# Second attention of a two-block transformer kernel: stationary values, outputs by feature, weights divided before their transposes

## The chip, the cores and the metric

The kernel runs on one core of one Trainium2 chip, as one launch. The metric is the device time of that launch in microseconds (us), taken as the median of several executions. Lower is better.

The engines are TensorE (PE in the profile; its weight loads are PEld), VectorE (DVE), ScalarE (ACT), GpSimd (POOL) and SyncE (SP), which only starts DMAs here. They run their own instruction lists, in the order of the program, and meet at semaphores.

## The reference

The program is a stack of two blocks over 512 tokens of 1024 features. This case is about the second attention of the first block, which comes after the first feed-forward network:

```python
kvf = rms_norm(h, kv_norm) @ w_kvf            # keys, values: 16 heads of 64; forget gates
c_sh = jnp.cumsum(log_sigmoid(kvf[..., 2 * B_WIDTH:] + b_f), axis=1)

def fox_mixer(xn, w_q, w_o, k, v, c):
    q = (xn @ w_q).reshape(B, T, B_HEADS, HEAD_DIM)
    for i in range(T // BLK):                 # BLK = 128 queries, keys up to the block's end
        s = q_block . k * scale + (c_q - c_k)
        s = jnp.where(causal, s, NEG)
        p = jax.nn.softmax(s, axis=-1)
        outs.append(p @ v[:, :q1])
    return concatenate(outs).reshape(B, T, B_WIDTH) @ w_o
```

All of it is float32. A dense product is made as three products of rounded parts (high by high, high by low, low by high); the products of softmax weights and values are plain float32.

## The kernel before, in words

**Layout.** Activations stand by feature: a tile of 128 partitions is 128 features, its 512 columns the tokens (KD = 8 such tiles make 1024 features). Scores stand by query: 128 queries in the partitions, up to 512 keys in the columns.

**Tasks.** The 16 heads go in 8 pairs. A pair has four tasks, one for each block `tb` of 128 queries, in the order 0, 2, 3, 1 (`MIXED`), which see 1, 3, 4 and 2 blocks of keys. That makes 32 tasks `t`. For each task and each of its two heads `g`:

- `pair_scores` (L1259, L1262): the scores of both heads, with the two heads on the two halves of the array's rows; results in banks 0 and 1.
- `pair_max` (L1326, L1330): VectorE adds the mask, takes the maximum and scales it.
- `pair_probs` (L1304): ScalarE takes the exponential and sums it. The weights are not divided yet.
- `pair_turn` (L1272): PE transposes the weights, a 128 by 128 block at a time, into banks 4 and 5. ScalarE copies head 0's (L1316), VectorE head 1's (L1351), into `b_PT`.
- `pair_values` (L1281): the transposed weights (128 keys by 128 queries) are the stationary operand and the values (128 keys by 64) the moving one. The result is by query, 128 by 64 a head, in bank 6 or 7.
- `pair_out` (L1335, L1337): VectorE takes the reciprocal of the sums and multiplies the result by it into `b_o`, which stands by token.

**Order on PE** (`b_pe`): in step t it runs the scores of task t+1, two blocks `k` of a key or query projection (`kq_fill`, half 0), the transposes of task t, two more blocks (`kq_fill`, half 1), and the values of task t-1. A block is three products of 128 by 128 by 512. `kq_fill` prepares the keys and queries of the next pair, two steps ahead (`KQ_AHEAD`), and has work in steps up to 25 only. VectorE and ScalarE follow the same steps; GpSimd makes the low part of each projection (L1244) and splits the weight units that come by DMA into a high and a low part (L497, L503). Three units fit into `parts`, so the split of a unit waits for the products of the unit three places ahead of it.

**After the last task** `flip_pe` (L1083) transposes `b_o` in 8 chunks of four blocks to stand by feature, `flip_act` (L1089) makes the high part and `flip_dve` (L1094) the low part (`b_fm`). Then `out_pe` makes the 8 output products of `w_o`, 24 matmuls each (L522 in all dense products); the first three are made together, block by block (`together=PARTS`), the others one after another. `out_dve` and `out_act` take them, form the norm and add to `h`.

**Ahead of the tasks** `mixb_pe` makes the first half of the values (`b_v0`), then `pre_sums_pe` (L653), which sums squares that VectorE has added (L663, L664), then the product of the forget gates (`b_f`, 24 matmuls), then `pre_columns_pe` (L676), which needs the reciprocal root (L657 on ScalarE, L669 on VectorE), then the second half of the values (`b_v1`), whose bank 7 comes free only after ScalarE's copy of those columns (L681).

## Time and profile before

| | us |
|---|---|
| median of 3 executions | 2281.19 |
| lowest, highest | 2278.80, 2281.82 |
| the profiled execution's own time | 2286.73 |
| its span, first to last instruction | 2284.9 |
| PE busy | 2157.0 (94%) |
| DVE, ACT, POOL busy | 1446.2, 591.0, 1157.0 |

The profile is of one execution. A span of an engine says that it worked, not that anybody waited for it. The chain of waits is followed back from the last instruction; "issue" in it is time in which the engine waited for nothing that the profile shows. The granted clock is that of TensorE, as a share of 2.4 GHz. The second attention, with what is ahead of it and its output products, takes the span from about 651 to 924 us.

### The profile page before, as it was taken

The page shows a single profiled execution, that of the slowest core. Times are in us where ns is not written, and L with a number is a line of the kernel's source. Part 1 is how long each engine was busy: PE and PEld are TensorE (multiplying, and loading weights), DVE is VectorE, ACT ScalarE, POOL GpSimd, SP SyncE. Part 2 cuts the span into 40 slices and gives each one's busy share as a digit, 9 for nine tenths or more (in the row PEclk, how much of TensorE's full clock was granted, in tenths as well). Part 3 has the DMA queues.
Part 4 walks back from the last instruction along what each step waited for, and adds up shares of the span by engine and source line. Part 5 has one row for each costly group of instructions (what it writes and reads, how often), then busy time and mean ns, then how long its engine had stood idle before and what let it go on. Part 6 is the DMA issues. An engine that isn't in the chain of part 4 may idle for free.

```text
span 2284.9 us, 34060 instructions
## 1 busy us (share of the span) xinstructions
PE 2157.0 (94%) x14118; PEld 1796.5 (79%) x14118; DVE 1446.2 (63%) x1894; ACT 591.0 (26%) x1215; POOL 1157.0 (51%) x658
## 2 busy tenths in 40 slices
PE   7999899999989998999999989989989978999998
PEld 5867788888868887788888758877888867888886
DVE  7455778567685454778767788768665664621622
ACT  2143321022133332321022142255434222200200
POOL 6711466765746443466665542543400354656654
PEclk9999999999989999999999999989989998999999
DMA  5310233532622111223433531112100112323321
GB/s 186 111 36 19 74 100 121 166 101 93 214 69 82 47 47 50 83 95 132 158 98 107 202 140 38 63 57 75 56 3 4 52 36 64 108 86 108 95 92 65
DMA packets 55769, 201.94 MB, mean 88 GB/s; under 512 B 6560, under 2 KB 6816, under 8 KB 54720
## 3 DMA queue, kind: packets, MB, share of 16 engines
q1 hardware_dynamic: 52272, 187.21, 25.2%
q0 software_dynamic: 1840, 9.60, 1.1%
q10 hardware_dynamic: 1504, 2.95, 0.5%
q8 instruction: 112, 1.84, 0.3%
q14 instruction: 41, 0.34, 0.0%
HBM read 194.76 MB, written 4.19 MB: 87 GB/s over the span
## 4 chain that ended last, share of the span: by engine, by line
PE 82%; DVE 11%; ACT 3%; issue 2%; POOL 1%; DMA 0%; SPq 0%; DVEq 0%; POOLq 0%; ACTq 0%
PE bank L522 64%; PE bank L1281 1%; PE bank L2636 1%; PE bank L988 1%; PE bank L2632 1%; PE bank L964 1%; DVE big L1513 1%; PE bank L2900 1%; PE bank L2621 1%; POOL parts_r L503 1%; PE bank L1709 1%; PE bank L1272 1%; PE bank L1521 1%; DVE big L663 1%; DVE h L798 1%
## 5 line engine op out<-in xcount | busy, mean ns | idle before, releaser
L522 PE MATMUL bank<-xn_r,parts_r 128*128 128x512 f32 (+1 forms) x2928 | 910.0, 390 | 32.0 <-DVE mix_r L746 13.2
L522 PE MATMUL bank<-big_r,parts_r 128*128 128x512 f32 x3208 | 926.9, 392 | 1.9 <-POOL parts_r L503 1.9
L503 POOL TENSOR_TENSOR parts_r<-ring,parts_r 128x1024 fp32r<-128x1024 f32 x293 | 739.9, 2525 | 24.4
L497 POOL TENSOR_SCALAR parts_r<-ring 128x1024 fp32r<-128x1024 f32 x293 | 346.5, 1182 | 792.5 <-PE bank L522 780.3
L522 PEld LDWEIGHTS bank<-big_r,parts_r 128*128 128x128 f32 x3208 | 603.0, 189 | 135.2 <-issue 5.7
L522 PEld LDWEIGHTS bank<-xn_r,parts_r 128*128 128x128 f32 x2928 | 551.5, 190 | 156.3 <-issue 35.2
L873 ACT ACTIVATE big<-bank,small 128x512 f32<-128x512 f32 x88 | 68.4, 780 | 411.0 <-DVE big L917 251.3
L902 DVE TENSOR_TENSOR bank<-bank,nb 128x512 f32<-128x512 f32 x88 | 61.3, 699 | 143.3 <-PE bank L522 143.2
L3167 DVE SCALAR_TENSOR_TENSOR h<-bank,vecs,h 128x512 f32<-128x512 f32 x24 | 17.9, 750 | 173.4 <-PE bank L522 173.4
L3241 DVE TENSOR_TENSOR big<-big 128x512 f32<-128x512 f32 x32 | 83.0, 2595 | 70.3 <-ACT big_r L3222 70.3
L533 DVE TENSOR_TENSOR big_r<-big,big_r 128x512 fp32r<-128x512 f32 x76 | 105.8, 1394 | 0.4
L522 PE MATMUL bank<-parts_r,xn_r 128*128 128x384 f32 x352 | 92.1, 343 | 6.5 <-ACT big L2025 3.5
L3046 POOL TENSOR_TENSOR big<-big 64x384 f32<-64x384 f32 x11 | 9.7, 878 | 158.6 <-PE bank L2664 147.3
L1513 DVE SCALAR_TENSOR_TENSOR big<-cst,vecs,big 128x1024 f32<-128x1024 f32 x42 | 88.0, 2122 | 2.5 <-DMA cst<-mod_w 1.6
L522 PE MATMUL bank<-mix_r,parts_r 128*128 128x512 f32 x208 | 82.0, 394 | 0.0
L917 DVE TENSOR_TENSOR big<-big 128x512 f32<-128x512 f32 x44 | 80.9, 1839 | 0.0
L3220 ACT ACTIVATE big<-bank 128x512 f32<-128x512 f32 x32 | 19.1, 597 | 220.1 <-PE bank L522 220.1
L522 PEld LDWEIGHTS bank<-parts_r,xn_r 128*128 128x128 f32 x352 | 64.9, 193 | 8.8 <-ACT big L2025 3.8
L910 DVE SCALAR_TENSOR_TENSOR big<-bank,small,big 128x510 f32<-128x510 f32 x88 | 65.9, 749 | 3.1
L696 ACT ACTIVATE nb<-mix 128x512 f32<-128x512 f32 x32 | 20.2, 632 | 175.3 <-DVE mix L786 105.4
L907 DVE SCALAR_TENSOR_TENSOR big<-bank,small,big 128x511 f32<-128x511 f32 x88 | 65.2, 741 | 0.5 <-ACT big L873 0.5
L522 PE MATMUL bank<-h_r,parts_r 128*128 128x512 f32 x160 | 63.1, 394 | 0.0
(443 smaller groups left out, 2901.8 us busy)
## 6 DMA issues: line engine op xcount, KB each, us to landing
ring<-weights SPq DMA_DIRECT2D x295, 512.0 KB, 3.5
cst<-mod_w SPq DMA_DIRECT2D x48, 512.0 KB, 4.1
cst<-consts SPq DMA_DIRECT2D x2, 1280.0 KB, 8.1
h<-x SPq DMA_DIRECT2D x8, 256.0 KB, 6.5
h_store<-h POOLq DMA_DIRECT2D x8, 256.0 KB, 2.3
big<-consts POOLq DMA_DIRECT2D x2, 1024.0 KB, 8.3
h<-h_store POOLq DMA_DIRECT2D x1, 2048.0 KB, 8.0
out<-mix SPq DMA_DIRECT2D x8, 256.0 KB, 2.2
```

What stands on the lines that cost most here:

```text
L497: pool.tensor_scalar(rounded(unit_parts(u)[0]), ring[:, u % RING], 1.0, 0.0, ALU.mult, ALU.add)\
L503: pool.tensor_tensor(rounded(lo), ring[:, u % RING], value(hi), ALU.subtract).then_inc(part_ready, 1)
L522: mm = pe.matmul(ps, rounded(w[a]), rounded(x[b]), start=(start and n == 0), stop=(stop and n == 2))
L533: dve.tensor_tensor(rounded(lo[:, k]), x[:, k], value(hi[:, k]), ALU.subtract).then_inc(sem(done), 1)
L663: link(dve, dve.tensor_tensor(pre_sq[:, 0:half], pre_sq[:, 0:half], pre_sq[:, half:2 * half], ALU.add))
L873: act.activation(cv[:, i % 4], bank[i % 4][:, :], ACT.Identity, bias=gain(f"cb{l}", 2 * KH * s + i), scale=gain(f"cw{l}2", 2 * KH * s + i))\
L902: dve.tensor_tensor(bank[i % 4][:, :], bank[i % 4][:, :], rstd, ALU.mult).then_inc(sem(st + "_sc"), 1)
L907: link(dve, dve.scalar_tensor_tensor(out=c[:, 1:T], in0=ps[:, 0:T - 1], scalar=gain(f"cw{l}1", w), in1=c[:, 1:T], op0=ALU.mult, op1=ALU.add))
L910: dve.scalar_tensor_tensor(out=c[:, 2:T], in0=ps[:, 0:T - 2], scalar=gain(f"cw{l}0", w), in1=c[:, 2:T], op0=ALU.mult, op1=ALU.add).then_in ...
L917: dve.tensor_tensor(ff_lo[:, j], ge[:, j % 2], cv[:, (2 * j + 1) % 4], ALU.mult).then_inc(sem(st + "_ff"), 1)
L1513: ins = dve.scalar_tensor_tensor(out=acc, in0=w, scalar=c, in1=acc, op0=ALU.mult, op1=ALU.add)
L3241: dve.tensor_tensor(ff2_lo[:, f], ff2_lo[:, f], ff2_lo[:, f], ALU.mult).then_inc(sem("mlp_sq"), 1)
```

## The change

1. **Values are stationary.** `pair_values` now takes the values (128 keys by 64) as the stationary operand and the transposed weights (128 keys by 128 queries) as the moving one. The two heads take the two halves of the array's columns, so that their results stand in partitions 0 to 63 and 64 to 127 of one bank, by feature. The four tasks of a pair write the four quarters of one bank (6 or 7 by turns).
2. **ScalarE divides ahead of the transposes.** A query is now a column of the result, so the division can't be made there. VectorE takes the reciprocal (`pair_norm`) right after its maximum of the same task, and ScalarE multiplies the weights by it in place (`b_scaled`), 128 by w a head, ahead of the transposes. `pair_out` is gone.
3. **No flip.** The 32 transposes, 8 high and 8 low parts behind the last task are gone. Each pair's bank is copied by ScalarE as it closes: pairs 0 to 5 (`B_STASH`) into `b_o`, since `xn` is in use until the last projection; their high parts are made by ScalarE in steps 26 to 28 and their low parts by GpSimd (`stash_lo_pool`); pairs 6 and 7 get their parts from ScalarE and VectorE directly.
4. **Output products start in the last steps.** `tail_fill` puts block k = t - 27 of output products 0 and 1 into steps 27 to 32, where `kq_fill` has nothing. The rest follows in `b_out_pe`, product after product; the three are no longer made together. GpSimd's split of unit 2 of `w_o` moves behind the six low parts.
5. **`b_f` ahead of `pre_sums_pe`.**

```diff
 def pair_turn(pe, t):
-    pe.wait_ge(*after("b_probs", 2 * t + g + 1))
+    pe.wait_ge(*after("b_scaled", 2 * t + g + 1))
 def pair_values(pe, t):
-    ps = grab(pe, 6 + t % 2, *after("b_rows", t + 1))
-    for g in range(2):
-        pe.wait_ge(*after("b_pt_dve" if g else "b_pt_act", t + 1))
-        for kb in range(tb + 1):
-            mm = pe.matmul(ps[:, g * HD:(g + 1) * HD], b_PT[t % 2][g][:, kb * P:(kb + 1) * P],
-                           b_v[:, kb, (2 * pair + g) * HD:(2 * pair + g + 1) * HD], ...)
+    if t % PAIR == 0:
+        grab(pe, 6 + pair % 2, *(after("b_stash", pair + 1) if pair < B_STASH else after("b_fm", pair + 1)))
+    ps = bank[6 + pair % 2]
+    pe.wait_ge(*after("b_pt_act", t + 1))
+    pe.wait_ge(*after("b_pt_dve", t + 1))
+    for kb in range(tb + 1):
+        for g, r in enumerate(half_rows):
+            mm = pe.matmul(ps[r, tb * P:(tb + 1) * P], b_v[:, kb, head * HD:(head + 1) * HD],
+                           b_PT[t % 2][g][:, kb * P:(kb + 1) * P], ...)
...
+def tail_fill(pe, t, half):
+    k = t - SPLIT_FROM - 1          # SPLIT_FROM = 26
+    if k >= 0:
+        b_out_product(pe, half, k)  # waits for b_fm k+1, then 3 matmuls
...
 def pair_probs(act, t):
     for g in range(2):
         act.activation(p_, p_, ACT.Exp, ..., accum_out=b_stat(t, 2)[:, g:g + 1])
+    act.wait_ge(*after("b_norm", t + 1))
+    for g in range(2):
+        act.activation(p_, p_, ACT.Copy, scale=b_stat(t, 3)[:, g:g + 1]).then_inc(sem("b_scaled"), 1)
...
+def pair_norm(dve, t):
     dve.wait_ge(*after("b_probs", 2 * t + 2))
-    link(dve, dve.reciprocal(b_stat(t, 3), b_stat(t, 2)))
-    dve.wait_ge(*after("b_values", t + 1))
-    dve.tensor_tensor(b_o[...], bank[6 + t % 2][:, 0:P], ..., ALU.mult)
+    dve.reciprocal(b_stat(t, 3), b_stat(t, 2)).then_inc(sem("b_norm"), 1)
 def b_dve(dve):
     for t in range(b_n):
         if t + 1 < b_n:
             pair_max(dve, t + 1)
+            pair_norm(dve, t + 1)
...
 # mixb_pe
-    pre_sums_pe(pe, "b")
     # product of b_f, 24 matmuls
+    pre_sums_pe(pe, "b")
     pre_columns_pe(pe, "b")
...
     b_pe(pe)
-    flip_pe(pe, "b", b_o, KD, "b_rows", lambda c: PAIR * (c + 1))
-    out_pe(pe, "b", "b_o", KD, b_oT, ("b_fm", 0))
+    b_out_pe(pe)
...
 # block.gpsimd
+    for pair in range(B_STASH):
+        stash_lo_pool(pool, pair)
-    split_units(pool, UNITS["b_kq"] + PARTS + 2 * KD, UNITS["hy"])
+    split_units(pool, UNITS["b_kq"] + PARTS + 2 * KD - 1, UNITS["hy"])
```

Three places show how the instructions stand. All line numbers of the kernel after are one to some eighty higher for the same code.

PE ahead of the tasks, from the last products of `b_v0` (parts_r as stationary of 128x512) on; 653 or 654 is `pre_sums_pe`, 676 or 677 `pre_columns_pe`, `big_r,parts_r x24` is `b_f`. Before:

```order
L522 MATMUL bank<-parts_r,big_r 128x512 x96
L653 MATMUL bank<-big,base 128x512
L522 MATMUL bank<-big_r,parts_r 128x512 x24
L676 MATMUL bank<-base,nb 128x1 x4
L522 MATMUL bank<-parts_r,big_r 128x512 x96
```

Now:

```order
L523 MATMUL bank<-parts_r,big_r 128x512 x96
L523 MATMUL bank<-big_r,parts_r 128x512 x24
L654 MATMUL bank<-big,base 128x512
L677 MATMUL bank<-base,nb 128x1 x4
L523 MATMUL bank<-parts_r,big_r 128x512 x96
```

The gates' product stands ahead of the sum of squares instead of behind it.

PE in step 29 of the tasks, from the scores of task 30 (512 keys) to those of task 31 (256 keys). Before:

```order
L1259 MATMUL bank<-nb_r,cst_r 128x512 x2
L1262 MATMUL bank<-big_r 128x512 x2
L1262 MATMUL bank<-xn_r,big_r 128x512 x2
L1262 MATMUL bank<-big_r,xn_r 128x512 x2
L1272 MATMUL bank<-base,big 128x128 x6
L1281 MATMUL bank<-big 128x64
L1281 MATMUL bank<-big,nb 128x64
L1259 MATMUL bank<-nb_r,cst_r 128x256 x2
```

Now:

```order
L1263 MATMUL bank<-big_r,xn_r 128x512 x2
L523 MATMUL bank<-xn_r,parts_r 128x512
L523 MATMUL bank<-big_r,parts_r 128x512
L523 MATMUL bank<-xn_r,parts_r 128x512
L1273 MATMUL bank<-base,big 128x128 x6
L523 MATMUL bank<-xn_r,parts_r 128x512
L523 MATMUL bank<-big_r,parts_r 128x512
L523 MATMUL bank<-xn_r,parts_r 128x512
L1286 MATMUL bank<-big 64x128
L1286 MATMUL bank<-nb,big 64x128
L1260 MATMUL bank<-nb_r,cst_r 128x256 x2
```

A block of output product 0 stands ahead of the transposes and one of output product 1 behind them; the values' results are 64 partitions by 128 columns instead of 128 by 64.

ScalarE in the tasks of one pair (1304 or 1338 the exponentials, 1316 or 1383 the copies of transposed weights, 1239 or 1240 a projection's high part). Before:

```order
L1304 ACTIVATE big,stat<-big,stat 128x128 x2
L1304 ACTIVATE big,stat<-big,stat 128x384 x2
L1316 ACTIVATE big<-bank 128x128
L1304 ACTIVATE big,stat<-big,stat 128x512 x2
L1316 ACTIVATE nb<-bank 128x384
```

Now:

```order
L1338 ACTIVATE big,stat<-big,stat 128x384 x2
L1343 ACTIVATE big<-big,stat 128x384 x2
L1383 ACTIVATE big<-bank 128x128
L1338 ACTIVATE big,stat<-big,stat 128x512 x2
L1343 ACTIVATE big<-big,stat 128x512 x2
L1383 ACTIVATE nb<-bank 128x384
L1240 ACTIVATE big_r<-xn 128x512
L1347 ACTIVATE big<-bank 128x512
```

Each task has two multiplications more (L1343), and each pair one copy of a whole bank (L1347).

## Rows read from the trace of the kernel before

**Rows 1.** Windows of PE: us, busy (instructions), granted clock, DMA share, GB/s.
```profile
657.00:662.00 5.00, 0.03 (x1) 0.82 0.15 59
...
664.00:667.00 3.00, 3.00 (x9) 0.50 0.03 10
```
**Rows 2.** The chain of waits ahead of the tasks: start, us, what.
```profile
661.97 2.05 PE bank L653 x2
664.01 6.94 PE bank L522 x24
670.96 0.80 PE bank L676 x8
...
672.93 39.96 PE bank L522 x168
```
**Rows 3.** The timeline of ScalarE and VectorE there, with idle time before.
```profile
664.05 0.69 ACT L657 ACTIVATE nb<-bank,small 128x512 f32<-128x512 f32 x1 [12.40 <-PE bank L653]
664.77 3.35 DVE L669 RECIPROCAL nb<-nb 128x512 f32<-128x512 f32 x1 [2.95 <-ACT nb L657]
```
**Rows 4.** The chain in the tasks of one pair.
```profile
776.42 1.73 PE bank L1281 x16
...
779.05 1.59 PE bank L522 x6
780.64 0.22 PE bank L1272 x2
780.86 1.39 PE bank L522 x6
782.25 0.84 PE bank L1281 x8
...
787.84 0.39 PE bank L1281 x4
...
792.74 1.28 PE bank L1281 x12
...
798.03 1.73 PE bank L1281 x16
```
**Rows 5.** The chain at two groups of f32 matmuls with 512 moving columns.
```profile
1316.88 1.82 PE bank L1685 x4
...
1581.51 1.00 PE bank L2374 x8
```
**Rows 6.** Groups by form in the tasks (712 to 878): busy us, mean ns | idle.
```profile
L1330 DVE TENSOR_SCALAR stat<-stat 128x2 f32<-128x2 f32 x32 | 19.0, 594 | 1.1
L1326 DVE CUSTOM_DVE_ANT_0 big<-bank,cst 128x512 f32<-128x512 f32 x16 | 10.4, 689 | 8.2 <-PE bank L1262 8.2
L1335 DVE RECIPROCAL stat<-stat 128x2 f32<-128x2 f32 x31 | 4.8, 154 | 0.0
L1304 ACT ACTIVATE big<-big,stat 128x512 f32<-128x512 f32 x16 | 11.4, 716 | 22.7 <-DVE stat L1330 22.7
L1239 ACT ACTIVATE big_r<-xn 128x512 fp32r<-128x512 f32 x14 | 8.8, 630 | 21.3 <-DVE xn L1234 21.3
```
**Rows 7.** PE's waits from 850 to 925 us: total, times, longest.
```profile
PE bank L522 <- POOL parts_r L503: 2.4, 1, 2.4
PE bank L1272 <- ACT nb L1316: 1.3, 1, 1.3
PE bank L522 <- DVE big_r L1094: 1.2, 1, 1.2
PE bank L1272 <- ACT big L1316: 0.9, 2, 0.5
```
**Rows 8.** The chain at the output products.
```profile
877.50 15.26 PE bank L522 x66
...
896.46 27.50 PE bank L522 x120
```
**Rows 9.** One line's instructions, durations min/median/max.
```profile
L1244 POOL TENSOR_TENSOR xn_r<-xn,big_r x16: 1272/1288/1298, 703.5 to 854.1; 128x512 fp32r<-128x512 f32 x16
```

## What the change would do, predicted before it ran

> **What bounds the kernel now.** PE is busy for 94% of the span, so I read the chain of waits first, and in the stretch that the change touches. It has three parts. *Ahead of the tasks* PE stands still: 5.1 us without work while VectorE adds squares, and the granted clock is at half (1.2 GHz) from 664 to 667 [rows 1]; the sum of squares, the gates' product at 0.289 us a matmul, the columns and the copy by ScalarE then follow each other until `b_v1` starts at 672.93 [rows 2]. *In the tasks* with projections to fill in (steps 0 to 25) the chain never leaves PE: the reader should see each row begin where the last one ends, and a pair come round in 798.03 - 776.42 = 21.6 us [rows 4]. ScalarE and VectorE wait there, so work on them is free as long as their own chain fits into PE's step. *In the tail* (steps 26 on, no `kq_fill`) PE waits: three times for copies of transposed weights, then 1.2 us for the low parts behind the flip, then 2.4 us for GpSimd's split of `w_o` unit 3, which could start only when product 0 closed, and product 0 closed late because the first three are made together [rows 7, 8].
>
> **Durations.** The sum is made against the profiled execution (2286.73 us, span 2284.9). The median, 2281.19, is 5.5 us (0.24%) lower; I take the difference of the sum off the median. A dense matmul on a warm clock is 27.50/120 = 0.229 us [rows 8].
>
> **Part 5, `b_f` ahead of the sum of squares.** Now PE idles from 657 to 661.97 [rows 1, 2]. With the change the 24 matmuls stand there at full clock: 24 x 0.229 = 5.5, to 662.5. The sum of squares took 2.05 on the low clock [rows 2], about 1.0 on the full one: 663.4. From there to the columns stand ScalarE's root (0.69) and VectorE's reciprocal (3.35) [rows 3]: 667.5. Then columns 0.8 and the same 1.2 to the start of `b_v1`: 669.5 against 672.93, a gain of 3.4. PE now idles 4.1 us there, which a half clock may follow. Before, half of `b_f` ran at it and is repaid already in the 5.5; a half clock over the first 3 us of `b_v1`, as long as the stretch in [rows 1], would give back 1.5, and twice that length 3. Bounds 0.4 and 3.4; I take **2.3**, nearer the upper one, since `b_v1` started on a lowered clock before as well.
>
> **Part 1, values.** Before, one logical product of 128x128 weights and 64 columns is two records of 0.107 us; a pair has 40 of them: 1.73 + 0.84 + 0.39 + 1.28 = 4.24 us [rows 4]. After, the moving operand has 128 columns. No row has this form. The bounds: a full f32 record with 512 columns takes 1.82/4 = 0.455, so one with 128 takes 0.114; eight records of the same 512 columns, on four narrow column groups over the same rows, took 1.00 us together instead of 3.6 [rows 5]. So column groups do run beside each other. Two heads side by side give 20 x 0.112 = 2.24 us a pair; one after the other 40 x 0.112 = 4.5. I take the first, since [rows 5] shows the overlap outright.
>
> There is a price. The same six dense matmuls take 1.39 us behind transposes and 1.59 behind the row-split scores [rows 4]: leaving a divided array costs 0.2 us. The change adds a second array shape to each step, so one more switch, x4 a pair = 0.8 us. Bounds for it 0.1 (only the drain, the gates small) and 0.3. So a pair costs 2.24 + 0.8 = 3.04 and gains 1.2.
>
> The Trainium skill speaks against this part: TensorEngine Tiling, Tiling Modes (Key Properties), says that changing the tiling mode drains the engine. By that rule, the trace agrees: 1.59 against 1.39. With a free change of mode this sum would be 6.4 us better over 32 tasks.
>
> With PE as the bound in 26 of 32 steps: 6.5 pairs x 1.2 = 7.8. At the start the first transposes wait for the reciprocal and two multiplications more, about 0.8. Together **7.0**. The bounds of the switch (0.1 and 0.3, that is 2.6 either way over 26 steps) go into the range.
>
> **Part 2, division.** ScalarE gets two multiplications a task. The nearest row is a copy out of SBUF of 512 columns, 0.63 [rows 6]; by width 0.63, 0.52, 0.41, 0.30, twice each, 3.7 us a pair, with a bank copy 4.3, on an engine that has a row's wait of 22.7 us ahead of the 512-key exponentials alone. Its load is hidden. The wait that is added is the question: VectorE now waits for the exponentials, with its copy for head 1 and `kq_take` queued behind; ScalarE waits for the reciprocal with its copy for head 0 behind. For a task with 512 keys, from the scores' end: hand-over 0.15; VectorE 2 x 0.69 + 0.17 = 1.5; exponentials 2 x 0.72; reciprocal 0.15 and 0.2 of hand-overs; multiplications 2 x 0.63: 4.9 us [rows 6]. PE meanwhile runs fill 1.6, transposes 0.7, fill 1.4, values 0.7, next scores 1.0, fill 1.6: 7.0 us, by rows like [rows 4]. It fits with 2.1 to spare. I cost it at nothing there; the cover is `kq_fill`. In the tail that cover is gone.
>
> **Parts 3 and 4, the tail**, from the scores of task 28 on. Work taken off PE: 32 transposes, 3.5 us; values of tasks 26 to 31, 6.9 to about 4.8 with their switches; against five switches back to dense products, 1.0. That is 4.6 less. The 192 output matmuls are the same 44 us, 36 of them moved forward. Waits taken off: all of [rows 7] and short ones at the flip, some 6. Waits added: ScalarE needs for each task of the tail its two exponentials, 0.36 for the reciprocal, two multiplications, one copy and up to two high parts, 3.5 to 5 us a step, where PE's step has 1.4 of fill now. The first tail block waits for the first low part: exponentials of task 27 (1.0), reciprocal (0.4), multiplications (0.8), copy (0.6), high part (0.6), then GpSimd's low part, 1.29 by [rows 9]: 4.7 us behind the end of the previous ScalarE step, of which PE covers 1.3 (scores and the end of values): wait 3.4. Steps 30 and 31 wait 2.2 and 1.8 for copies behind 512- and 256-key multiplications. Together 7.4. Unit 3 of `w_o` is split while products 1 and 2 run, so the 2.4 is gone. Net 4.6 + 6 - 7.4, about **3.2** gained. Behind the output products nothing changes but bank numbers.
>
> **Sum.** 2.3 + 7.0 + 3.2 = 12.5 us. Own time 2286.7 - 12.5 = 2274.2; median 2281.2 - 12.5, rounded to **2269**.
>
> **Rivals.**
>
> *Heads one after the other.* If the streams of two column groups didn't overlap, 20 slots a pair would be 40: 2.24 us more, x6.5 = 14.6, and 1.5 more in the tail where PE waits anyway: 2269 + 14.6 = 2283.6, no change within 0.2%. Against it is the 1.00 us in [rows 5]. 7%.
>
> *The division's chain becomes the bound.* VectorE's small multiply by the scale (L1330) took 0.594 us in the mean [rows 6] where its work is 0.17: something holds it up, by 0.4 in the mean, and GpSimd's ops of 1.3 to 2.4 us run beside it. In the trace this costs ScalarE time only, now it is in the chain. Say the chain is longer than 4.9 by x in every step. Below x = 2.1 only the six tail steps feel it, from there all. Break-even with before is at about 2.1 (6 x 2.1 = 12.6); slower by over 0.2% from about x = 2.3: 26 x 0.2 + 6 x 2.3 = 19, where 17 is needed. With x = 2.6 it is 26 x 0.5 + 6 x 2.6 = 28.6, the time 2298. For it speaks that three engines now hand over in turn; against it that x = 2.6 is six times the mean hold-up. 5%.
>
> The Trainium skill gives that hold-up a cause: SBUF — State Buffer, Who interferes with whom, says that VectorE in a two-port mode, which a `tensor_scalar` may enter, and GpSimd exclude each other for a whole instruction. By that rule, the mean of 0.594 agrees, and the added reciprocal (0.154 in the mean, never held up) does not add a second such place.
>
> *The tail gives its gain back.* More than 7.4 us of waits, or a clock at half after one or two of them, 1.5 us lost for each stretch as long as that in [rows 1], on top of longer waits: 2273 to 2277, and, if the blocks start no earlier at all and the change so doesn't do what it says, 2272. 22%.
>
> *Switches are cheap* (0.1) and `b_v1` starts warm: 3.2 more in the steps 0 to 31 and 1.1 ahead, with shorter tail waits: 2261 to 2264. 12%.
>
> *Forecast*: 2265 to 2273, 54%.
>
> **How the numbers follow.** The range must leave out at most 2 in 10. From 2261 to 2278 it holds the forecast, the cheap switches and the tail's case. Outside are the serial heads, the chain, and some overshoot. 0.2% is 4.6 us, about what a measurement of this kernel can tell from no change. Faster by more than that means under 2276.6: forecast, cheap switches and most of the tail's case, 0.85. Within it: serial heads and the rest of the tail's, 0.10. Slower: the chain, 0.05.
>
> **What the profile after would show.** Values: a block of keys in about 0.22 us instead of 0.43; a pair's period near 20.4 us instead of 21.6, with PE still in every row of the chain. Where `kq_fill` is, no PE wait for the transposes' inputs (releaser L1343); such rows there would be the second rival. Output block 0 waiting for GpSimd about 3 us. `b_v1` starting some 3 us sooner behind the last `b_v0` product. Between the last values and output product 7 no wait for GpSimd. The prediction is wrong if the pair's period stays at 21.6 or PE waits in the steps 0 to 25.

## The result, and the profile after

The changed kernel takes 2271.8 us (median of six, 2269.6 to 2274.5), the kernel before 2281.5 us (median of four). Executions over 1.5% longer than the fastest of their kernel (two of before, one of `e11`) are left out here and below. The recorded ratio is 0.9946, 95% interval 0.9921 to 0.9970: faster by 0.54%, some 12 us; the two medians alone are 9.7 us apart, a ratio of 0.9958, which lies in the same interval. The forecast was 2269 in a range from 2261 to 2278.

The profiled execution of after has a span of 2269.3 us, that of before 2284.9. By stretches, read from the starts of single matmuls, the 15.7 us lie here. ("Product" in the names is the last matmul of `b_v0` and of the output.) The columns: before, after, the difference, what the sum had, and the last kernel of the experiments (`e13`):

```
stretch                                     before   after   diff  forecast    e13
start -> last b_v0 product                  656.48  655.73   -0.8       0   655.29
-> first scores (gate, b_v1, first kq)       56.33   55.10   -1.2    -2.3    46.14
-> scores of task 28 (steps 0 to 26)        143.09  135.32   -7.8    -7.0   135.48
-> last output product (the tail)            67.66   63.71   -4.0    -3.2    58.99
-> first up product of ffn1                   9.36    8.43   -0.9       0     8.84
-> end                                     1352.02 1350.99   -1.0       0  1353.32
```

The sum had its 7.0 for the steps 0 to 25. The last row holds code that is the same in all kernels here. Over the profiles of this study it lies between 1345.1 and 1358.1 us, with no edit near it. So the experiments below are read from their stretches, and only `e11` and `e13`, with six executions each, also from times of whole runs.

First the chain of waits of after in a pair of the steady part; the columns are start, us, engine and line, `x` the instructions. It answers to [rows 4]. L1286 is `pair_values`, L523 a dense product; a record is one matmul as the trace lists it, and a product in plain float32 (f32) is two records:

```profile
751.67 1.02 PE bank L1286 x16
...
753.59 1.59 PE bank L523 x6
...
755.40 1.39 PE bank L523 x6
756.79 0.59 PE bank L1286 x8
...
762.13 0.37 PE bank L1286 x4
...
767.00 0.81 PE bank L1286 x12
...
771.81 1.02 PE bank L1286 x16
```

The values of a pair take 1.02 + 0.59 + 0.37 + 0.81 = 2.79 us, with their changes of array shape, against 4.24 before, and a pair comes round in 771.81 - 751.67 = 20.14 us instead of 21.6. The 1.45 us are the same in both readings, and the chain does not leave TensorE. The rows of 4, 8, 12 and 16 records take 0.37, 0.59, 0.81 and 1.02 us: each pair of records, one of either head, takes 0.109 us, and each row has 0.15 us on top.

The chain ahead of the tasks (it answers to [rows 2]), and windows there and in the tail (from:to, us, busy time and instructions of PE, PEld, DVE, ACT, POOL, then the granted clock, DMA share, GB/s), which answer to [rows 1]:

```profile
654.98 6.57 PE bank L523 x29
661.56 0.87 PE bank L654 x2
...
663.17 3.36 DVE nb L670
...
666.67 1.85 PE bank L677 x8
...
669.69 41.22 PE bank L523 x168
```
```profile
662.40:665.60 3.20, 0.01 (x1) 0.00 (x0) 2.43 (x1) 0.69 (x1) 2.63 (x2) 0.99 0.31 116
665.60:675.80 10.20, 7.94 (x23) 6.57 (x23) 3.93 (x9) 7.17 (x11) 0.00 (x0) 0.50 0.16 54
...
849.90:853.30 3.40, 3.40 (x10) 2.45 (x10) 0.42 (x1) 2.07 (x5) 1.46 (x2) 0.50 0.00 0
```

`b_f` now runs at full clock right behind the last `b_v0` product and covers the time in which VectorE adds the squares. Behind the sum of squares TensorE is idle for 4.3 us, and the clock is at half (1.2 GHz) for 10.2 us from 665.6 on. Before, it was at half from 660.2 to 667.0 and from 673.9 to 677.3, as long in sum.

TensorE's waits from 840 to 925 us (who waits, for whom: total, times, longest), where [rows 7] stood before:

```profile
PE bank L523 <- POOL big_r L1357: 3.0, 1, 3.0
PE bank L1273 <- ACT nb L1383: 2.4, 2, 1.9
...
PE bank L1273 <- ACT big L1383: 1.3, 1, 1.3
```

The chain shows how the longest comes about: division (L1343), copy of transposed weights (L1383), high part (L1353) and GpSimd's low part (L1357), and only then the early output product of step 27, which the half clock of 849.9 to 853.3 slows down:

```profile
846.85 0.49 ACT big L1343
847.34 0.48 ACT big L1383
847.82 0.53 ACT xn_r L1353
...
848.42 1.28 POOL big_r L1357
...
849.83 1.59 PE bank L523 x3
```

There is no wait for GpSimd's weight parts in the output products any more, as the sum had it. In the steps 0 to 25 two waits are left, 0.7 us at the scores of task 1, which before had too, and a new one of 0.5 us at the transposes of task 2; both stand ahead of the steady part.

### The profile page after: what moved, and what is told of

It reads as the page before. It is cut to its first block, busy times and chain, and to the rows that moved or that the text cites. A ratio compares the mean times of both kernels' runs of the same rounds, so it can differ in the third digit from the quotient of the medians.

```text
span 2269.3 us, 33969 instructions
## 1 busy us (share of the span) xinstructions
PE 2141.0 (94%) x14086; PEld 1767.4 (78%) x14086; DVE 1428.8 (63%) x1856; ACT 624.0 (27%) x1285; POOL 1163.3 (51%) x664
## 4 chain that ended last, share of the span: by engine, by line
PE 84%; DVE 8%; ACT 4%; issue 2%; POOL 1%; DMA 0%; SPq 0%; DVEq 0%; POOLq 0%; ACTq 0%
PE bank L523 68%; PE bank L2707 1%; PE bank L989 1%; PE bank L2971 1%; PE bank L2703 1%; PE bank L965 1%; POOL parts_r L504 1%; PE bank L2692 1%; PE bank L1286 1%; PE bank L1780 1%; PE bank L1592 1%; PE bank L1273 1%; PE bank L1792 1%; PE bank L1263 1%; PE bank L976 1%
## 5 line engine op out<-in xcount | busy, mean ns | idle before, releaser
L523 PE MATMUL bank<-xn_r,parts_r 128*128 128x512 f32 (+1 forms) x2928 | 918.4, 392 | 30.9 <-DVE mix_r L747 12.7
L523 PE MATMUL bank<-big_r,parts_r 128*128 128x512 f32 x3208 | 926.3, 392 | 2.2 <-POOL parts_r L504 2.2
L498 POOL TENSOR_SCALAR parts_r<-ring 128x1024 fp32r<-128x1024 f32 x293 | 341.7, 1166 | 769.1 <-PE bank L523 758.0
L523 PEld LDWEIGHTS bank<-big_r,parts_r 128*128 128x128 f32 x3208 | 602.4, 189 | 133.7 <-issue 4.7
L523 PEld LDWEIGHTS bank<-xn_r,parts_r 128*128 128x128 f32 x2928 | 555.6, 191 | 156.9 <-issue 37.3
L523 PE MATMUL bank<-parts_r,xn_r 128*128 128x384 f32 x352 | 89.8, 336 | 5.0 <-ACT big L2096 3.1
L523 PE MATMUL bank<-mix_r,parts_r 128*128 128x512 f32 x208 | 83.0, 399 | 0.0
L523 PEld LDWEIGHTS bank<-parts_r,xn_r 128*128 128x128 f32 x352 | 63.1, 188 | 6.9 <-ACT big L2096 3.4
L523 PE MATMUL bank<-h_r,parts_r 128*128 128x512 f32 x160 | 64.0, 400 | 0.0
```

Source lines behind the costliest of these rows:

```text
L498: pool.tensor_scalar(rounded(unit_parts(u)[0]), ring[:, u % RING], 1.0, 0.0, ALU.mult, ALU.add)\
L523: mm = pe.matmul(ps, rounded(w[a]), rounded(x[b]), start=(start and n == 0), stop=(stop and n == 2))
```

## The experiments

Twelve kernels ran. All but `e11` and `e13` ran once; their times, `e1` 2290.4 us, `e2` 2272.2, `e3` 2271.1, `e4` 2282.5, `e5` 2282.0, `e6` 2272.0, `e7` 2282.2, `e9` 2273.6, `e10` 2276.6 and `e12` 2270.6, move with the code that no edit touches and are not compared. Where a change is measured in a stretch, it is measured against the same stretch of the profile of after (of before for `e1`), and the names of the stretches are those of the table.

### The gate's product first, alone (e1)

```diff
-            pre_sums_pe(pe, "b")
             ps = grab(pe, 4, *after("b_z", 1))
             ... b_f, 24 matmuls ...
+            pre_sums_pe(pe, "b")
```
in the kernel before.

> The kernel before with one edit: TensorE multiplies b_f ahead of pre_sums_pe instead of behind it. All else is the kernel before. Theory (the gate edit alone gives what the changed kernel shows from the last b_v0 product to the first scores): from the last b_v0 product to the first b_v1 product 14.0 us instead of 16.45, and from there to the first scores 41.1 instead of 39.9, because the granted clock falls behind the wait for DVE's reciprocal instead of around b_f; together 55.1 instead of 56.3, about -1.2 us. Rival (the prediction's term): -2.3 us, 54.0 us together. Behind the first scores both expect the times of the kernel before: 210.8 us to the last output product, a pair in 21.6 us.

Measured: from the last `b_v0` product to `b_v1` 13.96 us, from there to the first scores 40.62, together 54.6 against 56.3 before: -1.7 us. Behind it all is as before (a pair in 21.57 to 21.61, 210.7 us from the first scores to the last output product). So the edit stands by itself, and what it gains and loses lies in this stretch alone. Up to `b_v1` it gains 2.5 us here, in after and in every kernel whose gate is that of after. How much of this `b_v1` gives back depends on the length of the half clock: 0.7 us in `e1` and 1.3 in after, where it lasts 10.2 us. In `e2`, whose gate is that of after, it lasts 6.8 us (666.3 to 673.1), nothing is given back, and the stretch takes 53.7 us. So the edit brings between 1.2 and 2.7 us.

### Heads one after the other (e2)

```diff
-            for kb in range(tb + 1):
-                for g, r in enumerate(half_rows):
+            for g, r in enumerate(half_rows):
+                for kb in range(tb + 1):
```

> The changed kernel with the two loops of pair_values exchanged: all blocks of head 0, then all of head 1, so neighbouring matmuls use the same column half of the array. Theory (the two heads' matmuls run side by side because they stand on different column halves, and that is the gain on the values): the values of a pair take about 2 x 2.24 us instead of 2.8 with their switches, so some +2.0 us on a pair: a pair every 22.1 us instead of 20.14, and the stretch from the first scores to the last output product about 15 us longer, 214 us instead of 199. Rival A (the gain comes from 64-wide stationary loads and a moving width of 128 alone, whatever the order): a pair stays at 20.1 us. Rival B (part of the wait at the switch is hidden once matmuls of one half queue up): +1.0 us on a pair, 207 us.

The chain of waits in the same steps:

```profile
746.62 1.07 PE bank L1286 x12
...
751.71 1.51 PE bank L1286 x16
...
757.30 0.59 PE bank L1286 x8
...
762.64 0.37 PE bank L1286 x4
```

A pair takes 20.91 us, 0.77 more than after, and the stretch from the first scores to the last output product 204.7 instead of 199.0. That is neither the full 2.0 of the theory nor nothing. The rows tell why: with 4 and 8 records the time is that of after (0.37, 0.59), with 12 it is 0.26 longer and with 16 it is 0.49 longer. A record of one half of the columns follows the last of the same half after 0.109 us. The single records show head 1's first one starting at 752.13 us, while head 0's last three of eight, which stand ahead of it in the program, are still to start; from there both halves take one each in 0.109 us. Four records of either head run side by side in every task, however long its streams are: 16 records then take 12 steps instead of 8 (4 x 0.109 = 0.44 more), 12 take 8 instead of 6 (0.22), 8 and 4 lose nothing. The overlap of the two halves is shown, and so is its reach in this order: some four records. Rival B came nearest, with a part hidden and 1.0 us a pair.

### No division (e3)

```diff
-            act.wait_ge(*after("b_norm", t + 1))
-            for g in range(2):
-                ... act.activation(p_, p_, ACT.Copy, scale=...).then_inc(sem("b_scaled"), 1)
...
-                pe.wait_ge(*after("b_scaled", 2 * t + g + 1))
+                pe.wait_ge(*after("b_probs", 2 * t + g + 1))
```

> The changed kernel without the division of the weights: the two scaled copies of a task on ScalarE are left out, and the turn of a head waits for its exps alone (the result is not divided by the row sums). Theory (the chain exps, sums, reciprocal, scaled copies is hidden in the steady state, where it had 2.1 us to spare, and costs only where a task has no cover, at the first task and in the last six steps): a pair stays within 0.1 us of 20.14; the first turn comes some 1.5 to 3 us sooner; the last steps give back up to 3 us; in all 2 to 6 us less from the first scores to the last output product (193 to 197 us instead of 199). Rival (the chain paces each step): a pair falls by 4 x 0.5 us or more, to 18 us or less, and the stretch to under 187 us.

The kernel leaves the weights undivided. Measured: a pair in 20.14, not changed by 0.01. The first pair takes 15.90 instead of 16.64; the whole stretch 194.9 instead of 199.0, so the division costs 4.1 us: 0.7 at the start, nothing in the steady steps, 3.4 in the tail. TensorE's waits from 830 to 925 us:

```profile
PE bank L523 <- POOL big_r L1353: 2.9, 1, 2.9
...
PE bank L1273 <- ACT nb L1379: 0.3, 1, 0.3
PE bank L1273 <- ACT big L1379: 0.2, 1, 0.2
```

The waits for copies fall from 3.7 to 0.5 us, but that for the first low part stays: it is not the division's.

### A longer division (e4, e5)

```diff
             act.wait_ge(*after("b_norm", t + 1))
+            for n in range(3):                       # e5: range(8), 64 columns each
+                act.activation(var[:, n * 128:(n + 1) * 128], base[:, 0:128], ACT.Copy)
             for g in range(2):
```

> The changed kernel with three extra copies of 128 columns (constants into an unused buffer) on ScalarE in each task, between the wait for the reciprocal and the scaled copies; a scaled copy of 128 columns takes 0.39 us, so the chain of every task is about 1.1 us longer. Theory (the chain has about 2 us to spare in each steady step): a pair stays at 20.14 us; the start and the last six steps, which have no cover, grow by 1.1 us for each step that waits today, 3 to 6 us in all, so that the stretch from the first scores to the last output product is 202 to 205 us instead of 199. Rival (the chain is at its limit already): a pair grows by about 4.4 us, the stretch to over 225 us.

Measured: a pair in 20.14, the stretch 203.9 us (+4.8). The dose was smaller than I had reckoned: the copies follow each other on ScalarE every 0.21 us, so three of them add 0.62 us to a task, not 1.1.

> The changed kernel with eight extra copies of 64 columns on ScalarE in each task at the same place, some 0.3 us each, so 2.4 us or a little more on every task's chain, above the spare of about 2.1 us that the trace of before was read for. Theory: the steady steps begin to wait, a pair takes 21 to 23.5 us instead of 20.14, and the stretch from the first scores to the last output product is 210 to 230 us. Rival (the spare is much more than 2.1 us, the reading of it was too careful): a pair stays at 20.14 us and only start and end grow, to 206 to 209 us.

Eight copies of 64 columns follow each other every 0.15 us and add 1.19 us to a task, not 2.4. Still a pair takes 20.51 us, 0.37 more, and the stretch is 207.6. So the theory's verdict (the steady steps begin to wait) came at half the dose that it named, and 2.1 us is not what the steps have to spare. The chain of waits of this kernel at the one step in a pair that grew, that of the 512-key task:

```profile
764.03 1.12 ACT nb L1342 x7
765.15 1.23 ACT big L1345 x2
766.38 0.38 ACT nb L1385
...
766.81 1.09 PE bank L1273 x8
```

L1342 are the added copies, L1345 the division, and L1385 is ScalarE's copy of the *previous* task's transposed weights. The next transposes write into the bank that this copy empties. It stands in ScalarE's queue behind the exponentials and the division of the next task. That path has less time to spare than the division's own. The same place in the timeline of after (start, us, engine, line):

```profile
763.19 0.47 ACT L1383 ACTIVATE nb<-bank 128x384 f32<-128x384 f32 x1
```

It ends at 763.66, and the transposes (L1273) begin at 764.59: 0.93 us to spare, the least of the four steps of a pair; the next is 1.60, ahead of the transposes of the 384-key task. The division of head 0 ends at 762.67, 1.92 us ahead of the same transposes, so the 2.1 us were read nearly rightly for the chain that they were read for. 1.19 us more leave a wait of 0.26, and the single matmuls show 0.28 at this place and, with 0.06 and 0.02 behind it, the 0.37 of the pair; the other three steps are unchanged. Only 0.10 us of the wait is idle time of TensorE, as the record of the matmul ahead of it covers the rest, and the list of waits doesn't have it; the chain and the period tell it.

### One change of shape more (e6)

```diff
+                if t >= 1 and t < SPLIT_FROM:
+                    pair_values(pe, t - 1)
                 kq_fill(pe, t, 1)
                 tail_fill(pe, t, 1)
-                if t >= 1:
+                if t >= SPLIT_FROM:
                     pair_values(pe, t - 1)
```

> The changed kernel with the values of a task ahead of the second key and query fill instead of behind it, in the steps ahead of the last pair: the values then stand between the transposes and a fill of another array shape, and the next scores behind that fill, so that TensorE changes its array shape once more in a step. Theory (each change of shape costs 0.2 us as the prediction took): 25 steps, +5 us: a pair 20.9 us instead of 20.14, the stretch 204 us. Rival A (a change costs nothing of its own): 20.14 us and 199 us. Rival B (the values then wait for the copies of their own step's predecessor, which are due by then anyway): no wait shows at the values in either case, and where one shows it is told apart by its row.

```profile
751.95 1.02 PE bank L1286 x16
752.98 1.60 PE bank L523 x6
...
755.47 1.59 PE bank L523 x6
```

The six dense matmuls behind the values now take 1.60 us, as those behind the scores do, where behind transposes they took 1.39. A pair takes 20.97 us on average, 0.83 more for four changes, 0.21 each, and the stretch 205.2 us (+6.2, 1.1 of it in the tail's waits for GpSimd, which rose from 3.0 to 4.1). The price of 0.2 us stands for this change, from the divided shape back to 128 by 128. The rule of the Trainium skill (TensorEngine Tiling, Tiling Modes, Key Properties) that a change of tiling mode drains the engine names the same thing; by that rule, the trace agrees, at 0.21 us for this change. The change that the kernel after really adds stands elsewhere, between a dense product and the scores of the next task, and the rows of the values show 0.15 us for it.

### All output products behind the last task (e7)

```diff
 def tail_fill(pe, t, half):
-            if k >= 0:
+            if k >= KD:
                 b_out_product(pe, half, k)
...
 def b_out_pe(pe):
-            for k in range(B_STASH, KD):
-                for f in range(B_EARLY):
-                    b_out_product(pe, f, k)
-            for f in range(B_EARLY, KD):
+            for f in range(KD):
```

> The changed kernel without output products in the last steps: all 64 of the output's block products come behind the last task, one output block after the other; values, division and the early high and low parts are as in the changed kernel. Theory (the products in steps 27 to 32 fill time in which TensorE would wait for the task chain, which without them is as long as in the kernel before): the last steps lose their cover and the stretch from the first scores to the last output product grows by 5 to 9 us, to 204 to 208 us. Rival (the tail is paced by the number of TensorE instructions, since the chain has 2.1 us to spare): within 1 us of 199. The 3.0 us wait for POOL's low part is gone in either case, as all low parts are ready by then.

```profile
PE bank L1273 <- ACT big L1380: 5.2, 3, 2.6
PE bank L1273 <- ACT nb L1380: 2.9, 3, 1.9
```

Measured: 199.7 us, 0.7 more than after. That was a miss: I had expected 5 to 9. The fill is gone and TensorE waits 8.1 us for ScalarE's copies instead of 3.7, but the wait of 3.0 for GpSimd is gone with it. In the changed kernel, beginning the output products early brings next to nothing, 0.7 us. What the tail gains over before must come from the rest: the flip and its waits, the shorter values and the 2.4 us wait for unit 3 of `w_o`, which `e7` doesn't have either. How it divides among them was not tried.

### High and low parts earlier (e9)

```diff
-        b_oT = (xn, b_o)
+        b_oT = (b_xkv[0], b_o)
...
-                if SPLIT_FROM <= t < SPLIT_FROM + B_STASH // 2:   # two a step from step 26
+                if 0 <= t - 24 < B_STASH:                         # one a step from step 24
...                                                          # GpSimd: low part 0 ahead of kq_lo(15),
                                                              # one weight unit behind low part 1
```

> The changed kernel with the high and low parts of the first six output blocks made earlier: ScalarE writes the high parts into the buffer that the key products leave free at step 24, one a step from step 24 (instead of two a step from step 26 into the buffer of the query input), and GpSimd makes the first low part ahead of the low part of the last query unit and splits one more weight unit behind the second. Theory (the first early output product waits 3.0 us for GpSimd's low part alone): that wait is gone, the half clock behind it too, and the early products cover the chain as meant; the stretch from the first scores to the last output product is 195 to 196 us instead of 199. Rival (the wait only moves to the turn of the same step, which waited behind it): 198 us or more, with waits of 1 us and more for ScalarE's copies in the place of the one that went.

The stretch is 197.4 us, 1.7 less. The wait for GpSimd is gone and the clock stays at 1.00 from 840 to 860 us. The scores of task 31 begin 147.5 us after the first ones instead of 150.8. Then half of the gain goes again:

```profile
860.60 1.30 POOL big_r L1358
...
861.99 0.06 DVE big_r L1368
862.05 0.55 issue
862.60 0.41 DVE big L1403
...
866.37 1.12 PE bank L1273 x4
```

The half clock comes here, from 866.0 to 869.5. High part 5 was made in step 29. GpSimd's low part 5 follows it (860.60), VectorE's low part of output block 6 waits for that (861.99), and VectorE's row maxima of the next task stand behind it in the queue (L1403, 862.60), so TensorE waits 2.8 us for that task's transposes. The rival came half true: the wait moved, by way of a queue that neither theory had named.

### Filler in the gate's wait (e10)

```diff
             pre_sums_pe(pe, "b")
+            keep_busy(pe, 6, 14)
             pre_columns_pe(pe, "b")
```

> The changed kernel with 14 filler matmuls (128x256, 0.29 us apart by the rows of the program's other fillers, 4.1 us) between pre_sums_pe and pre_columns_pe, where TensorE waited 4.26 us for DVE's reciprocal. Theory (the granted clock fell to half from 665.6 to 675.8 us because TensorE was idle for those 4.3 us, and the 10.2 us at half clock cost most of what part 5 was to bring): the clock stays at 1.0 through the stretch; from the last b_v0 product to the first scores 50 to 52.5 us instead of 55.1. Rival (the half clock comes whatever TensorE does, as another kernel stretch drew on the same budget before): it stays half for about 10 us somewhere in the stretch, and the sum is 55 us.

A miss, and one of my own making. The timeline of TensorE:

```profile
666.93 8.00 PE L483 MATMUL bank<-base 128*128 128x256 f32 x28 [4.45 <-DVE vecs L1619]
```

The filler waited itself, 4.45 us, for VectorE's sums of the modulation vectors: they read bank 6 and stand in VectorE's queue behind the reciprocal. So TensorE was idle as before, the filler came on top (28 records in 8.0 us, where I had reckoned 4.1), and from the last `b_v0` product to the first scores it took 61.0 us. On the clock this run says nothing: it fell, but there was an idle stretch.

### Products of b_v1 in the gate's wait (e12), and both (e11)

```diff
             pre_sums_pe(pe, "b")
-            pre_columns_pe(pe, "b")
-            tm_linear(pe, "b_v1", ...)
+            for k in range(3):                 # b_v1: token blocks 0 and 1, banks 5 and 6
+                for i in range(2):
+                    block(i, (k,))
+            pre_columns_pe(pe, "b")
+            ... k = 3 of blocks 0 and 1, then blocks 2 and 3, then k = 4 to 7 of all ...
```

> The changed kernel with real work in that wait in place of fillers: the first three steps of b_v1 for the first two token blocks (18 matmuls, 4.1 us) ahead of pre_columns_pe, the fourth behind it, where TensorE waited 1.2 us for ScalarE to empty the bank of the fourth block, then the other two blocks; the number of matmuls is that of the changed kernel. Theory: both waits (4.3 and 1.2 us, 5.4 of the 14.0 us) are filled and the clock stays up: from the last b_v0 product to the first scores 45 to 48 us instead of 55.1, with a program's end 7 to 10 us earlier where the rest is alike. Rival A (weights: the units come by GpSimd's split and are not there so early): a wait for GpSimd's parts of 2 us or more takes its place, 50 us or more. Rival B (the kq parts behind are bound by the split of their units, not by TensorE): the gain is given back at the first scores, 52 us or more.

```profile
663.37 5.30 PE L523 MATMUL bank<-parts_r,big_r 128*128 128x512 f32 x15 [3.75 <-DVE vecs L1656]
```

The same bank 6 holds it up for 3.75 us; only the three matmuls on bank 5 ran in the wait. Still the stretch falls to 51.3 us from 55.1: the 1.2 us wait for the bank of block 3 is covered, 0.5 us of the idle time is gone, and the half clock lasts 3.4 us (664.9 to 668.3) instead of 10.2, which was not foreseen and which this run doesn't explain. In `e11` the same code has 6.8 us of it. Rivals A and B both fall: no wait for weights, and the gain is still there at the first scores.

`e11` has these products and, in place of `e9`'s order, the high parts of blocks 0, 1, 2 in steps 24, 25, 26 and of 3, 4, 5 in step 27.

> The changed kernel with the products of e12 in the gate's wait, and with the early high and low parts of e9 in another order: the high parts of output blocks 0, 1 and 2 at steps 24, 25 and 26, and of 3, 4 and 5 at step 27, where ScalarE was idle for 2 us. In e9 the part of block 5 stood in step 29, GpSimd's low part behind it, and DVE's low part of block 6 behind that, with the row maxima of a task queued behind it on DVE: 3.3 us were gained up to there and 1.7 were left. Theory: the stretch from the first scores to the last output product is 195 to 196 us instead of 199.0 (e9: 197.4), and from the last b_v0 product to the first scores it is 45 to 48 us; by both 9 to 13 us less than the changed kernel, 2259 to 2263 us. Rival (both gains stand, but the time behind them moves by as much as it does from run to run with the clock): within 5 us of the changed kernel's 2271.8.

```profile
PE bank L1273 <- ACT big L1384: 2.2, 3, 1.3
...
PE bank L1273 <- ACT nb L1384: 1.3, 2, 0.7
```

From the first scores to the last output product 194.5 us, 4.6 less than after and 2.9 less than `e9`: the wait behind low part 5 is gone, and the clock is at 1.00 from 850 to 890 us. Against `e7`, where all output products stand behind the last task, it is 5.2 us. `e11` has the early output products and the parts in time for them, `e7` neither; what each brings by itself was not tried. The gate's stretch is 52.2 us. The median is 2264.2 us, the ratio to before 0.9909 (0.9888 to 0.9930).

### Bank 6 free in time (e13)

```diff
 def pre_recip_dve(dve, st):
             pre_add_dve(dve, st)
+            if st == "b":
+                mod_out(dve, 0)
             dve.wait_ge(pre_sd_ready, PRES.index(st) + 1)
             dve.reciprocal(rstd, var)
```
and no `mod_out` behind it, else `e11`.

> The kernel of e11 with one edit on DVE: the sums of the modulation vectors (mod_out, 0.33 us, which read bank 6) are done ahead of the reciprocal, where DVE waits 2.0 us for ScalarE's square root, and not behind it. In e10, e12 and e11 TensorE waited 3.8 to 4.5 us at the first matmul into bank 6 for just these sums, which stood in DVE's queue behind the 3.35 us reciprocal, so that it was idle in the gate in all three and the granted clock fell in all three. Theory (the idle stretch brings the half clock, and the filler products are worth what the wait was): TensorE is never idle over 0.5 us from the last b_v0 product to the first scores, the clock stays at 1.0 there, and the stretch is 45 to 46.5 us instead of 52.2 (e11) and 55.1 (the changed kernel); 5.5 to 7 us less than e11 in all, about 2259 us. Rival A (the clock falls there even without an idle stretch): 1 to 3 us of it stay, 47 to 49 us. Rival B (another reader holds the filler back, as the sums did): a wait of 1 us or more with another name on it, 48 us or more.

The timeline of TensorE, and windows with the granted clock (third column from the right):

```profile
660.96 1.02 PE L654 MATMUL bank<-big,base 128*128 128x512 f32 x2
661.41 4.68 PE L523 MATMUL bank<-parts_r,big_r 128*128 128x512 f32 x18
666.31 1.02 PE L679 MATMUL bank<-base,nb 128*128 128x1 f32 x8 [0.21 <-DVE nb L672]
```
```profile
662.00:666.00 4.00, 4.00 (x18) 3.01 (x17) 3.19 (x1) 0.69 (x1) 2.66 (x2) 1.00 0.33 110
666.00:676.00 10.00, 9.79 (x48) 8.18 (x48) 4.29 (x8) 8.54 (x13) 4.25 (x3) 1.00 0.13 48
```

18 products fill the wait, 0.21 us of it is left, and the clock stays at 1.0. The stretch takes 46.1 us instead of 52.2 (`e11`), 55.1 (after) and 56.3 (before). The theory's number held: the half clock came with the idle stretch and went with it. The median is 2259.0 us (2253.6 to 2263.3), the ratio to before 0.9887, 95% interval 0.9860 to 0.9915, below the interval of the changed kernel (each against its own runs of before). This version beats both kernels.

## Why the prediction was right, point by point

**What bounds.** Right: in the steady steps the chain never leaves TensorE, before and after. The one new wait in the steps 0 to 25, 0.5 us in step 2, belongs to the start, for which the sum had 0.8.

**Part 5, forecast 2.3, measured 1.2 (after), 1.7 (`e1`) and 2.7 (`e2`).** The mechanism was right, its size was taken from too short a half clock. Up to `b_v1` the sum had 3.4 us and 2.5 are there: the missing 0.9 are the columns, 1.85 us at half clock behind the idle stretch, where the sum had 0.8 at full. Behind that it took a half clock of 3 to 6 us, as long as the stretch of [rows 1] or twice that, and it was 10.2 in after, 6 of them in `b_v1` itself. The window of [rows 1] was a part only: before was at half for 6.8 us around it and for 3.4 us more from 673.9, so the edit moved as long a half clock as there had been. `e13` against after shows what the idle time, the clock and the 1.2 us wait for a bank cost together: 9.0 us.

**Part 1, forecast 1.2 a pair, measured 1.45; forecast 7.0, measured 7.8 up to step 26.** The mechanism was right and is shown (`e2`, `e6`). The sum had 2.24 us of records and 0.8 of shape changes, 3.04; measured are 2.18 and 4 x 0.15 = 0.6, 2.79. The price of 0.2 was read behind the scores, where a divided shape is left for 128 by 128, and `e6` confirms it for such a change (0.21); the added change of this kernel is another one and costs 0.15. The start was forecast at 0.8 and cost 0.7 (`e3`).

**Part 2, at nothing in the steady steps: right** (`e3`, `e4`), **but the spare was wrong.** It was put at 2.1 us from the division's own chain, whose terms add up to 4.7 us and not to the 4.9 of the sum; the trace of after has 1.92 us on that chain. The path that is short is another one, ScalarE's copy of the previous task's transposed weights, with 0.93 us (`e5`). The prediction named this copy as "behind" the wait, and did not work its time out. The rival that rested on this spare, the chain as the bound from x = 2.1 on, would have begun at 0.9 in one step of four and at 1.6 in a second, so its 5% rested on a number twice too kind. It also weighed the mean hold-up of VectorE's small multiply (0.4 us), while single ones were longer: in before those of tasks 9, 17 and 25 lasted 2.41 us each, that is 2.2 us held up. In after none lasts over 0.79 us in the tasks 3 to 27. Nothing in the prediction said that they would shrink, so part of this term at nothing is luck.

**Parts 3 and 4, the tail, forecast 3.2, measured 4.0.** The waits came as forecast in place and somewhat shorter: 3.4, 2.2 and 1.8 us against 3.0, 1.9 and 1.3; one of 0.5 stands ahead of the tail, in step 26. What had been left out of the sum is the half clock from 849.9 to 853.3 behind the first of them. What was not seen is that the early products pay for nothing but their own wait (`e7`). The 2.4 us of [rows 7] are gone, as forecast; that it was the making of three products together that held unit 3 back was read from the trace and not tried by itself.

**The rivals.** *Heads one after the other*: not so, and `e2` shows that even in that order a pair would have lost 0.77 us and not 2.24; the price of this rival was wrong by a factor of three. *The tail gives its gain back*: half true. Its mechanism, a half clock behind a wait, is there: the three rows behind the wait take 1.59, 0.85 and 1.22 us, where the same work at full clock takes 0.89, 0.44 and 0.70, 1.6 us more in all. The waits were 1.2 us shorter than in the sum, which hid most of it. And `e7` shows that part 4 alone gave back nearly all of its own gain. *Cheap switches*: half way, 0.15 where the sum had 0.2 and the rival 0.1; and `b_v1` did not start warm.

**The sum.** 12.5 forecast; 1.2 + 7.8 + 4.0 = 13.0 in the stretches that the change touches. That they agree so closely is luck in part: one part came out 1.1 us short and the other two 0.8 over each. In the profiles another 2.7 us differ outside of them: 0.9 is a half clock in the sums of the norm behind the output (1.72 us at L646 before, 1.17 at L647 after), and the rest lies in code that no edit touches and that moves by more from run to run.

## What to carry to other kernels

Work that is put ahead of a wait is only worth what its own inputs allow: look for the last of them, the bank it writes and whose queue frees that bank, before counting it as cover. The spare time of a chain is that of the shortest path through every queue that its instructions stand in, the copy of the task before among them, not that of the chain alone. Where a dense engine goes idle for some microseconds, reckon with the half clock behind it as a price of its own, and fill the gap with real products first.

## What the runs showed of the hardware

- Two 64-column halves of the array take matmuls of two streams side by side, and the second stream may be queued behind the first: some four records of it run beside the first stream's last ones, and its first one starts ahead of three that stand before it in the program. 16 records of f32 with 128 moving columns took 1.02 us with the heads alternating, 1.51 in turn (`e2`).
- An f32 record with 128 stationary and 64 moving columns followed the last every 0.107 us in before (1.73 us for 16), one with 64 stationary and 128 moving columns every 0.109 us on its half of the columns in after: half of the moving columns saved nothing.
- Six dense matmuls take 1.59 to 1.60 us behind a shape with divided rows or divided columns and 1.39 behind a 128 by 128 one: 0.21 us for going back to the whole array (`e6`). Values with divided columns between a dense product and scores with divided rows take 0.15 us on top of their records.
- The same code with the same idle time of some 4.3 us ahead of it was followed by 10.2 us at half clock in after and by 6.8 in `e2`.
- VectorE's small multiply ahead of the exponentials (L1407, work 0.17 us) takes 0.37 us in the mean, once 1.74 us at the start and once 1.15 in the tail, and in before 0.594 in the mean and up to 2.41; all ten that last over 0.25 us in after have an instruction of GpSimd beside them. The reciprocal of the same size (L1411) takes 0.17 in the mean and is never held up. The Trainium skill (SBUF — State Buffer, Who interferes with whom) gives a port shared with GpSimd, which a `tensor_scalar` may lock, as the cause; by that rule, the trace agrees, and no run here tried it alone.
- ScalarE's copies of 64 and 128 columns last 0.24 and 0.29 us, but follow each other every 0.15 and 0.21 us (`e5`, `e4`): a load made of them is smaller than the sum of its durations.
